# A two-block sequence kernel on one core: PSUM slots, a wait and the order of eight products changed

## What is computed

```python
# first block (one layer)
z = rmsnorm(h, norm1_g)
q, fl, iv, og, pin, ga, gb = split(z @ w_in)
o_a = hgrn2_mixer(q, fl + b_f, iv, og, lb, head_g)      # gated recurrence, 8 heads
o_b = pool_mixer(pin, w_pool, pool_scale)
mix = sigmoid(ga) * (o_a @ w_branch_a) + sigmoid(gb) * (o_b @ w_branch_b)
h = h + mix @ w_out
z = rmsnorm(h, norm2_g)
u, v = split(z @ w_up)                                  # 2 x 2816 columns
h = h + (silu(causal_dwconv(u)) * v) @ w_down
h = rmsnorm(h, final_norm_g)
# second block (one layer): u = rmsnorm(h) @ w_in_2, split in eleven parts, then
#   latent attention (cq, ckv, k_pe, z_mla) and attention with forget gates (fq, fk, fv, f_logit, z_fox)
mixed = (sigmoid(gate_a) * y_mla + sigmoid(gate_b) * y_fox) @ w_out_2
h = h + rmsnorm(mixed, post_norm_g)
```

## Time and profile before

| | |
|---|---|
| time, median of 3 runs | 1572.91 us (1572.83 to 1573.08) |
| the profiled execution | 1572.91 us, span 1571.1 us |
| TensorE matmul busy | 1533.6 us, 98% |
| weight loads into TensorE busy | 1349.0 us, 86% |
| VectorE busy | 838.2 us, 53% |
| ScalarE busy | 694.2 us, 44% |
| memory traffic | 79 GB/s over the span |
| mean granted TensorE clock | 0.994 of full speed |

### The profile page before, as it was taken

One profiled execution on the slowest core, in us unless ns is written; L12 is line 12 of the kernel. 1 busy time (PEld: TensorE's weight loads), 2 busy tenths in 40 slices (PEclk: granted clock), 3 DMA queues, 4 the chain that ended last, 5 costly groups with the idle time before them and its releaser, 6 DMA issues.

```text
span 1571.1 us, 24012 instructions
## 1 busy us (share of the span) xinstructions
PE 1533.6 (98%) x10287; PEld 1349.0 (86%) x10287; DVE 838.2 (53%) x1234; ACT 694.2 (44%) x1036; POOL 3.6 (0%) x16
## 2 busy tenths in 40 slices
PE   7999999999999999999999899999999999999998
PEld 7999999999998998998888667778899778778888
DVE  6467766645645665653345576542222556543343
ACT  6555676654333222322323655542223666643232
POOL 0000000000000000000000000000000000000000
PEclk9999999999999999999999999999999999999999
DMA  6212112114332222222234100123232111122322
GB/s 229 81 61 82 54 55 68 56 41 150 97 106 81 99 90 93 96 85 99 94 94 109 27 28 1 55 81 107 81 95 67 55 54 55 54 67 81 107 81 81
DMA packets 130541, 125.46 MB, mean 80 GB/s; under 512 B 20169, under 2 KB 128484, under 8 KB 130052
## 3 DMA queue, kind: packets, MB, share of 16 engines
q1 hardware_dynamic: 129956, 120.36, 24.3%
q0 software_dynamic: 464, 3.56, 0.6%
q10 hardware_dynamic: 16, 0.00, 0.0%
HBM read 119.66 MB, written 4.26 MB: 79 GB/s over the span
## 4 chain that ended last, share of the span: by engine, by line
PE 87%; DVE 6%; ACT 4%; issue 2%; DMA 0%; SPq 0%; DVEq 0%; ACTq 0%
PE PS L841 73%; PE PS L953 3%; PE PS L1167 2%; PE PS L1110 2%; DVE wlo L1784 2%; PE PS L1132 2%; DVE small L2301 1%; ACT Pm L1296 1%; ACT xka L1296 1%; ACT whi L1296 0%; PE PS L1144 0%; PE PS L1115 0%; DMA xt<-in_x 0%; PE PS L965 0%; PE PS L1116 0%
## 5 line engine op out<-in xcount | busy, mean ns | idle before, releaser
L841 PE MATMUL PS<-zhi,whi 128*128 128x258 f32 (+2 forms) x1872 | 486.7, 320 | 6.1 <-DVE zlo L1830 3.4
L841 PE MATMUL PS<-zlo,whi 128*128 128x258 f32 (+2 forms) x1872 | 475.4, 314 | 0.0
L841 PE MATMUL PS<-zhi,wlo 128*128 128x258 f32 (+2 forms) x1872 | 475.1, 314 | 0.0
L841 PEld LDWEIGHTS PS<-zhi,whi 128*128 128x128 f32 x1872 | 309.0, 190 | 30.7 <-issue 5.7
L841 PEld LDWEIGHTS PS<-zhi,wlo 128*128 128x128 f32 x1872 | 307.6, 189 | 21.4
L841 PEld LDWEIGHTS PS<-zlo,whi 128*128 128x128 f32 x1872 | 307.6, 189 | 18.9
L1784 DVE TENSOR_TENSOR wlo<-raw,whi 128x2048 fp32r<-128x2048 f32 (+2 forms) x114 | 247.8, 2174 | 112.4 <-ACT whi L1296 112.0
L1296 ACT ACTIVATE whi<-raw 128x2048 fp32r<-128x2048 f32 (+2 forms) x114 | 207.4, 1819 | 149.6 <-DMA raw<-in_w_up 55.7
L1296 ACT ACTIVATE Pm<-PS,small 128x144 f32<-128x144 f32 (+3 forms) x128 | 68.6, 539 | 79.2 <-DVE small L2301 79.2
L2301 DVE TENSOR_REDUCE small<-PS 128x1 f32<-128x144 f32 (+3 forms) x128 | 62.5, 502 | 37.6 <-PE PS L1117 36.9
L841 PE MATMUL PS<-ghi,whi 128*128 128x512 f32 x176 | 69.6, 396 | 0.0
(11 more groups left out here) (351 smaller groups left out, 2155.4 us busy)
## 6 DMA issues: line engine op xcount, KB each, us to landing
raw<-in_w_in SPq DMA_DIRECT2D x50, 1024.0 KB, 5.1
raw<-in_w_up SPq DMA_DIRECT2D x22, 1024.0 KB, 5.1
raw<-in_w_out SPq DMA_DIRECT2D x8, 1024.0 KB, 5.3
raw<-in_w_down SPq DMA_DIRECT2D x8, 1024.0 KB, 5.1
raw<-in_w_br_mla SPq DMA_DIRECT2D x4, 1024.0 KB, 5.3
raw<-in_w_br_fox SPq DMA_DIRECT2D x4, 1024.0 KB, 5.3
raw<-in_w_down SPq DMA_DIRECT2D x4, 768.0 KB, 4.7
hspill<-hT SPq DMA_DIRECT2D x1, 2112.0 KB, 8.6
```

What stands on the lines that cost most here:

```text
L841: ins = mm(o_, l_, r_, start=first, stop=last)
```

## The change

Four things differ. The plan gives other PSUM slots to u1, kpe, cq, mv and fin. The gate units of k 4 to 7 now all stand ahead of all branch units of `("y", 1, k)`, in the plan and on TensorE, with the weight splits on ScalarE and VectorE re-ordered to match. `mixlo` is computed one product late throughout. TensorE waits for all 22 tiles of `g` at once ahead of the down products, where the first column pair waited step by step.

```diff
@@ make_plan
-    def two(names, w, col0, x, kt=KT, mode="full", slots=(0, 1)):
+    def two(names, w, col0, x, kt=KT, mode="full"):
...
-            pl.piece(name, u, 128 * i, kt, x, mode, slot=slots[n % 2])
+            pl.piece(name, u, 128 * i, kt, x, mode, slot=n % 2)
...
-    for x in range(2):
-        gate(1, 2 + x)
-        for j in range(2):
-            branch(1, 2 * x + j)
+    for j in range(2, 4):
+        gate(1, j)
+    for j in range(4):
+        branch(1, j)
...
-        two([("u", 2 * j), ("u", 2 * j + 1)], "w_up", 256 * j, "z", mode="late", slots=(0, 1 if j else 2))
+        two([("u", 2 * j), ("u", 2 * j + 1)], "w_up", 256 * j, "z", mode="late")
...
     for i, name in enumerate((("ckv", 0), ("kpe", 0))):
-        pl.piece(name, u, 128 * i, KT, "z", "full", slot=2 * i)
+        pl.piece(name, u, 128 * i, KT, "z", "full", slot=i)
...
-        pl.piece(("cq", i), u, 128 * i, KT, "z", "full", slot=(1, 0)[i])
+        pl.piece(("cq", i), u, 128 * i, KT, "z", "full", slot=(2, 0)[i])
...
-            pl.piece(("mv", i, j), pl.ukv, j, 1, "ckv", "values", slot=(2, 1, 0)[(2 * i + j) % 3], k0=i)
+            pl.piece(("mv", i, j), pl.ukv, j, 1, "ckv", "values", slot=(1, 2, 0)[(2 * i + j) % 3], k0=i)
...
-            pl.piece(("fin", j, i), u, 0, KT, "mx", "tokens", slot=(2, 0, 1)[n % 3], k0=i)
+            pl.piece(("fin", j, i), u, 0, KT, "mx", "tokens", slot=n % 3, k0=i)
@@ TensorE
-            for x in range(2):
-                for k in (4 + 2 * x, 5 + 2 * x):
-                    gemm(("g", 1, k))
-                pe.wait_ge(oa_ready, 4)
-                for k in range(4 * x, 4 * x + 4):
-                    gemm(("y", 1, k))
+            for k in range(4, KT):
+                gemm(("g", 1, k))
+            pe.wait_ge(oa_ready, 4)
+            for k in range(KT):
+                gemm(("y", 1, k))
...
+            pe.wait_ge(g_ready, FT)
             for j in range(4):
...
-                        gemm(("dn", 2 * j + m), None if j else g_ready)
+                        gemm(("dn", 2 * j + m))
@@ ScalarE
-            w_high(U(("y", 1, 0)), U(("y", 1, 2)))
-            high_at = {0: ("g", 1, 6), 2: ("y", 1, 4), 3: ("y", 1, 6), 4: ("out", 0), 7: ("out", 2)}
+            w_high(U(("g", 1, 6)), U(("y", 1, 0)))
+            for k in range(4, KT):
+                tile_done(act, ("g", 1, k))
+                tile_free(A_(halves(late(ga(k))), acc_late(("g", 1, k)), ACT.Sigmoid), ("g", 1, k))
+                if k == 5:
+                    w_high(U(("y", 1, 2)))
+            w_high(U(("y", 1, 4)))
             for k in range(KT):
-                if k % 4 == 0:
-                    for x in (4 + k // 2, 5 + k // 2):
-                        tile_done(act, ("g", 1, x))
-                        tile_free(A_(halves(late(ga(x))), acc_late(("g", 1, x)), ACT.Sigmoid), ("g", 1, x))
                 act.wait_ge(mix_ready, k + 1)
                 A_(late(mixhi[:, k, :]), late(mix[:, k, :]), ACT.Copy).then_inc(mixhi_ready, 1)
-                if k in high_at:
-                    w_high(U(high_at[k]))
+                if k in (3, 5, 7):
+                    w_high((U(("y", 1, 6)), U(("out", 0)), U(("out", 2)))[k // 2 - 1])
@@ VectorE
-            w_low(U(("y", 1, 0)), U(("y", 1, 2)))
-            low_at = {1: (("g", 1, 6),), 3: (("y", 1, 4), ("y", 1, 6)), 5: (("out", 0),)}
+            w_low(U(("g", 1, 6)), U(("y", 1, 0)))
+            w_low(U(("y", 1, 2)))
             for k in range(KT):
...
-                if k % 4:
+                if k:
                     mix_lo(k - 1)
-                if k % 4 == 3:
-                    mix_lo(k)
-                w_low(*(U(n) for n in low_at.get(k, ())))
+                if k in (1, 4, 6):
+                    w_low({1: U(("y", 1, 4)), 4: U(("y", 1, 6)), 6: U(("out", 0))}[k])
+            mix_lo(KT - 1)
             w_low(U(("out", 2)))
```

## The result

| | before | after |
|---|---|---|
| time, median of 5 runs | 1573.08 us (1572.83 to 1574.34) | 1581.0 us (1578.91 to 1584.73) |
| ratio of after to before | | 1.0057 (1.0043 to 1.0073) |
| the profiled execution | 1572.91 us, span 1571.1 us | 1581.14 us, span 1579.3 us |
| mean granted TensorE clock | 0.994 | 0.995 |

The change makes the kernel slower. Between the medians of five runs the difference is 7.9 us. All 15 executions of the changed kernel on record average 1582.2 us (1578.6 to 1584.9), 9.0 us or 0.57% above the 1573.3 us that the five of the kernel before average, and that is the ratio of the table. The forecast was 1579.3 us with a range of 1577.2 to 1581.6 us: the median of five lies inside the range, 1.7 us above the forecast, and the mean of 15 lies 0.6 us above the top of it. So the direction came as forecast, and something is missing from the sum.

A forecast was written before the change was run, and what follows sets the result against it. TensorE, busy 98% of the span, was taken to bound the kernel, so its new stalls add to the time: 1.6 + 1.16 + 1.15 + 2.5 = 6.4 us on 1572.9 gives 1579.3 us, range 1577.2 to 1581.6.

The forecast's parts named there:

- Part 1: Gate and branch products reordered: late weight splits on VectorE stall y6 and delay the first output pair, +1.6 us.
- part 1 costs nothing: Rival: the splits fit between the y products and TensorE waits for y7's tmp as before; 1577.7 us, chance 0.11.
- Part 2: Pair u0/u1: u1 in slot 1 makes the pair wait until VectorE has taken out7 from it, +1.16 us.
- part 3: Pair ckv/kpe: kpe in slot 1 makes the pair wait until VectorE has added dn7, +1.15 us.
- Parts 4 and 5: Slots of cq and mv, and of fin, where one of the first pair takes slot 1 either way: 0 us each.
- Part 6: Down products: TensorE waits for all 22 tiles of g instead of step by step, +2.5 us.
- the waits themselves cost: Rival: removing 44 single-step waits ahead of down products gives time back, 1569.8 us or less; chance 0.03, including misread order.
- Within 0.2%: Rival: pair waits are overlapped, parts 1, 2 and 3 cost nothing, only the 2.5 us wait remains; 1575.4 us, chance 0.06.
- TensorE's clock enters here: Step noting that holes between matmul bursts can drop the clock to 1.2 GHz; 1.00 across today's hole at 417 us.
- The granted clock 1.00 in 480 to 860 us: Sign expected in the changed profile: TensorE's granted clock stays at 1.00 over that stretch.
- The rival had this mechanism: Rival: the clock falls after the new hole at 716 us, at most 3.4 us lost; 1582.7 us, chance 0.08.
- The sign of being wrong: Wrong if: y6 unstalled, output-pair hole no wider, matmuls twice as long after the down-product hole, or mark distances elsewhere changed.

The follow-up runs named there:

- The earlier splits: Kernel before with the new gate and branch order, but the weight splits for y6/y7 and out0 one branch product earlier: 1574.33 us, ratio 1.0.
- the better version: Kernel before with out1 in slot 2 and fin's counter set so its first pair misses slot 1: 1571.87 us, ratio 0.9985.
- the filled kernels: Kernel before with the wait for g, or that plus a split wait, the hole filled with unread matmuls: 1575.85 us and 1579.06 us.
- the one of 4.9 us: Kernel before with the wait for g and for the second down unit's weight split ahead of the down products, unfilled: 1581.83 us, ratio 1.0048.

## Why the prediction was right, and where not

- **Part 1, +1.6.** Right, +1.59 and +1.60 in the changed kernel's two traces and +1.60 with the order alone. Its two steps too: the stop at y6 was 0.54 us (forecast 0.68, because TensorE started 0.05 us behind the split's end and not 0.2), and y7's `tmp` started at 420.17 (forecast 419.25; this trace runs 0.95 us later from its first 350 us on). The earlier splits took all of it away. The rival "part 1 costs nothing" is out.
- **Part 2, +1.16, and part 3, +1.15.** Right: +1.11 and +1.13 with the slots alone, and +1.12 at u0/u1 in the changed kernel's second trace. At ckv/kpe the changed kernel has +1.25 in both traces; the 0.1 us more isn't explained.
- **Parts 4 and 5, 0.** Right. Fin's first pair has slot 1 under either counter and TensorE is idle ahead of it under both; the better version, whose first pair has slots 2 and 0, has no wait there.
- **Part 6, +2.5.** Right: +2.39 alone, +2.43 in the changed kernel. The 44 single waits that went away give nothing back: the stretch behind them takes 123.79 and 123.77 us in the filled kernels without them, 123.72 with them. So the rival "the waits themselves cost" is out. "Within 0.2%" is out too: parts 1, 2 and 3, which it put at nothing, each cost what the forecast said within 0.1 us.
- **The sum, 6.4.** 1.59 + 1.12 + 2.43 + 1.25 = 6.4 by the traces.
- **The step that failed is "TensorE's clock enters here", which the sum took as nothing.** The range had 0.6 us for it at its top. "The granted clock 1.00 in 480 to 860 us" held in the traces of the changed kernel, but the clock fell at 422, ahead of that window. The argument was that a hole of 1.5 us at 417 left the clock at 1.00. It does; part 1 makes it one of 2.65 us between matmul starts, and behind holes of that length the runs show the clock at half for 3.4 us in some executions and at 1.00 in others. Of six such holes traced (the changed kernel twice, two each; the order alone; the wait for g alone) two were followed by the low clock. The rival had this mechanism, at the down products only, with a chance of 0.08 and a price of 3.4 us. It measured 1.6 us each time it struck. Over the executions of the changed kernel the excess over 6.4 is 0.6 us in the second set (the five beside the experiments) and 2.6 us in the first 15 (1582.24 less 1573.26, the mean of before's five runs, less 6.4; 1.8 us against before's mean over all its executions, 1574.1). A term of two holes at a third each and 1.6 us, +1.1, would have given 1580.4, so 1.8 us of the 1582.2 would still be missing. The first set goes with the clock: its six executions at a mean granted clock of 0.995 or more average 1580.0 us, the nine at 0.991 to 0.994 average 1583.8. These have no trace, except one, so at which places the clock fell in them, and whether it accounts for all of the excess, stays open.
- **The sign of being wrong.** Besides the matmuls of twice the duration, which did come behind this hole in one trace of the wait for g alone, the forecast named a change of distance between marks outside the edited places. That came: the first 350 us and the 640 us ahead of fin changed in every later trace. The account of the waits didn't fail by it, since they change in kernels without an edit there as well; that a trace of the same work moves by up to 2.6 us there wasn't foreseen.
- **What the Trainium skill made of it.** The section the forecast named (TensorE: Matmul & The Clock Gate, "HAM oscillation — how this bites in real kernels") says that holes between bursts of matmuls drop the clock. The traces agree in part: two of the six unfilled holes of 2.6 us were followed by the lower clock, 1.6 us lost behind each, and four weren't; the one of 4.9 us was, with 2.69 us lost. The forecast gave the rule too little.
- **The base.** Three runs within 0.25 us suggested that the kernel before hardly scatters. Its 74 executions beside the experiments lie between 1572.5 and 1576.9 us with a standard deviation of 1.2 (mean 1574.1), and those at a mean granted clock of 0.997 or more average 1573.0, those at 0.992 to 0.994 average 1574.8. So part of that scatter goes with the clock. Against the one trace of before, the first 350 us take 0.5 to 2.6 us more in all later traces, with no edit there in any kernel, and the 640 us ahead of fin 0.1 to 1.0 us less in those that keep the wait at fin. What makes these differ was not settled. At the value products around 880 us the granted clock is seen to fall in some traces (0.57 on the mean from 874 to 882 us in that of before, 0.79 from 882 to 890 us in the changed kernel's, which is 9 us later by then).

## What to carry over

Where two products run as a pair, both slots' waits stand ahead of the first matmul: look up, with the counter's real value, who had each slot last, and give the second product one that has long been free. Where an in-order engine both splits weights and empties PSUM, keep a long split out of the time just before the last result that the next pair needs. And price a new hole in TensorE's work with more than its length: ask what the clock does behind it, carry that as a chance with a price, and take more than three runs before deciding how much a kernel scatters.

## What was not expected of the hardware

- A hole of 2.6 us between matmul starts in otherwise unbroken work left the granted clock at 1.00 in one execution and at half for 3.4 us in another of the same kernel; both times it fell the products behind it took 1.6 us longer. With 4.9 us it was down in the one trace taken (2.69 us lost).
- Matmuls whose result nobody reads kept it at 1.00 in all the filled holes traced, at no cost in the holes that they fit (the waits were as long as unfilled, within 0.02 us at the output pair and at the down products). Among the value products the stretch with them took 0.85 us more (40.81 against 39.96, one trace each).
- 44 waits on a semaphore that was already high cost TensorE nothing that the marks show (123.72 us with them, 123.77 and 123.79 without).
